# Twenty attention heads in one sequence, the memory rows split by GpSimd, and the recurrence's keys and turns moved

## The reference, cut to what matters

```python
# first block
proj = rms_norm(h) @ w_in                        # attention, gating unit, gates
h = h + merged @ w_out
h = h + hier_moe(rms_norm(h), ...)               # 32 experts of width 256; two for each row
x = rms_norm(h, norm_f_g)
# second block: two layers over x, with a memory of 256 rows
mem_n = rmsnorm(mem, mem_norm_g)
for layer in (0, 1):
    u = rmsnorm(h, norm_g[layer, 0])
    mem_kv = mem_n @ w_mem_kv[layer]
    # layer 0: 16 heads of 64 with a window and a sink; layer 1: a gated recurrence of 8 heads, in chunks of 16
    o = mixer(u)
    c = memory_cross_attn(xq, mem_kv)            # 4 heads of 128, in both layers
    h = h + rmsnorm(concatenate([o, c]) @ w_out)
    h = h + rmsnorm(conv_ffn(rmsnorm(h)))
```

## Time and profile before

| what | value |
|---|---|
| median of 3 runs | 1323.81 us |
| lowest and highest run | 1322.87 and 1324.84 us |
| the profiled execution's own time | 1322.58 us |
| its span, first to last instruction | 1320.9 us |
| instructions | 18486 |
| PE, PEld busy | 1236.1 and 988.4 us |
| POOL, ACT, DVE busy | 770.3, 659.5 and 483.7 us |
| moved by DMA | 275.01 MB |

### The profile page before, as it was taken

The page is one execution under the profiler, slowest core; times in us unless marked ns, Lnnn a source line. Parts: engine busy times, 40 slices in busy tenths (PEclk is TensorE's granted clock), DMA queues, the critical chain, the costliest instruction groups (busy, mean ns, idle before and its releaser), DMA issues.

```text
span 1320.9 us, 18486 instructions
## 1 busy us (share of the span) xinstructions
PE 1236.1 (94%) x7264; PEld 988.4 (75%) x7264; DVE 483.7 (37%) x1084; ACT 659.5 (50%) x1148; POOL 770.3 (58%) x345
## 2 busy tenths in 40 slices
PE   8999999999888778999899999999999889999998
PEld 6888877777343333888788888888998678888986
DVE  2527343433121111456603444102458281344411
ACT  6455544653111011745646666545798443666651
POOL 5778985440000000982176888996688905788894
PEclk8999999998999999999999999999999999999999
DMA  6745554298999999562143655653534413355561
GB/s 210 259 138 187 191 186 159 100 366 334 422 421 375 422 422 413 177 221 81 33 150 113 206 181 184 237 190 128 191 128 169 167 65 128 129 191 192 191 204 67
DMA packets 127037, 275.01 MB, mean 208 GB/s; under 512 B 6580, under 2 KB 55020, under 8 KB 115180
## 3 DMA queue, kind: packets, MB, share of 16 engines
q1 hardware_dynamic: 126668, 272.86, 56.6%
q10 hardware_dynamic: 288, 1.05, 0.2%
HBM read 272.85 MB, written 1.05 MB: 207 GB/s over the span
## 4 chain that ended last, share of the span: by engine, by line
PE 75%; DMA 8%; ACT 7%; DVE 4%; POOL 3%; issue 2%; SPq 1%; DVEq 0%; ACTq 0%; POOLq 0%
PE lin_ps L950 11%; PE lin_ps L952 11%; PE lin_ps L951 11%; DMA ring<-in_w_expert_in 7%; PE lin_ps L1003 6%; PE sc_ps L1268 4%; POOL w_low L877 3%; PE lin_ps L1005 3%; PE tr_ps L1003 3%; PE sc_ps L1003 3%; PE lin_ps L980 2%; PE lin_ps L983 2%; PE lin_ps L982 2%; ACT w_high L1568 2%; PE lin_ps L1088 2%
## 5 line engine op out<-in xcount | busy, mean ns | idle before, releaser
L877 POOL TENSOR_TENSOR w_low<-ring,w_high 128x1024 fp32r<-128x1024 f32 (+1 forms) x318 | 761.0, 2429 | 456.0 <-ACT w_high L1568 456.0
L1568 ACT ACTIVATE w_high<-ring 128x1024 fp32r<-128x1024 f32 (+1 forms) x320 | 313.8, 1043 | 102.1 <-PE lin_ps L952 32.7
L950 PE MATMUL lin_ps<-w_high,x_span 128*128 128x512 f32 (+2 forms) x432 | 168.6, 390 | 5.1 <-POOL w_low L877 2.6
L951 PE MATMUL lin_ps<-w_low,x_span 128*128 128x512 f32 (+2 forms) x432 | 166.2, 385 | 0.0
L952 PE MATMUL lin_ps<-w_high,x_low 128*128 128x512 f32 (+2 forms) x304 | 116.5, 383 | 0.0
L1003 PE MATMUL lin_ps<-x_span,w_high 128*128 128x512 f32 x320 | 112.6, 397 | 1.5 <-ACT work L1598 1.5
L950 PEld LDWEIGHTS lin_ps<-w_high,x_span 128*128 128x128 f32 x432 | 81.7, 189 | 21.8 <-DVE w_low L2115 2.8
L951 PEld LDWEIGHTS lin_ps<-w_low,x_span 128*128 128x128 f32 x432 | 81.8, 189 | 15.2
L980 PE MATMUL lin_ps<-x_span,w_high 128*128 128x256 f32 x320 | 91.4, 286 | 0.0
L982 PE MATMUL lin_ps<-x_span,w_low 128*128 128x256 f32 x320 | 90.5, 283 | 0.0
L1005 PE MATMUL lin_ps<-x_span,w_low 128*128 128x256 f32 x320 | 89.3, 279 | 0.0
(11 more groups left out here) (465 smaller groups left out, 2371.7 us busy)
## 6 DMA issues: line engine op xcount, KB each, us to landing
ring<-in_w_expert_in SPq DMA_DIRECT2D x30, 2048.0 KB, 16.0
ring<-in_ffn_w_in SPq DMA_DIRECT2D x44, 1024.0 KB, 7.4
ring<-in_w_in SPq DMA_DIRECT2D x12, 2048.0 KB, 7.8
ring<-in_b_w_in SPq DMA_DIRECT2D x11, 2048.0 KB, 8.1
work<-in_w_expert_out SPq DMA_DIRECT2D x8, 2048.0 KB, 23.3
ring<-in_w_expert_out SPq DMA_DIRECT2D x8, 2048.0 KB, 22.4
ring<-in_ffn_w_out SPq DMA_DIRECT2D x8, 2048.0 KB, 7.8
ring<-in_a_w_in SPq DMA_DIRECT2D x4, 2048.0 KB, 8.0
```

The source lines that it names most:

```text
L877: pool.tensor_tensor(w_low[:, slot, 0:words], raw, w_high[:, slot, 0:words].bitcast(F32), ALU.subtract).then_inc(low_made, 1)
L950: pe.matmul(out[:, t, :], high(k)[:, at], wh[:, j, :], start=(k == 0), stop=False)
L951: pe.matmul(out[:, t, :], high(k)[:, at], wl[:, j, :], start=False, stop=False)
L1568: act.activation(w_high[:, slot, 0:words], raw, ACT.Copy).then_inc(high_made, 1)
```

## The change

It does four things.

1. **One sequence.** The sixteen heads and the four of cross attention become one sequence of twenty on PE, ACT and DVE. The split of two units moves behind the turn of head 19.
2. **The memory rows.** ACT copies the turned rows in full to one place, `mem_T`. DVE's eight subtractions go. POOL copies `mem_T` to `mem_high` and subtracts, once batch 1's first weights are used, and PE waits for that (`mem_split`) before `kv00`. PE's wait for all eight chunks moves into `w_out1`, ahead of its third chunk. Since `mem_high` isn't there yet, `keep_running` takes `ident` by `ident`, 128 columns, 64 and 26 times. The place of `mem_high` holds one more 1 MB load until then: expert 4's half of batch 1's part a=1, issued ahead of the second half of batch 0's.
3. **The keys.** The fourth level place moves to `gain`. ACT moves the near keys of the first pair before it copies b2 and b3. SP loads the next `gain` only after all sixteen level products, and what stands behind it in SP's queue waits too. PE waits for the block in the banks of the levels first, and for the other one ahead of the chunks.
4. **The turns.** Heads 6 and 7 are turned ahead of chunks 3 and 5 of `o10`.

The diff, cut to its core:

```diff
-        mem_high, mem_low = overlay("mem_high", 6 * 2048, [P, KC, SEQ]), overlay("mem_low", 9 * 2048, [P, KC, SEQ])
+        mem_high, mem_low = overlay("mem_high", 9 * 2048, [P, KC, SEQ]), overlay("mem_low", 6 * 2048, [P, KC, SEQ])
...
+        mem_T = feat(buf(6))
...
-        level_at = [(work, 0), (work, 1024), (attn, 0), (attn, 1024)]
+        level_at = [(work, 0), (work, 1024), (attn, 0), (gain, 0)]
...
+        later_slot = buf(9).rearrange("p (k n) -> p k n", k=4)
...
             def load_gain(src, uses_before):
+                if uses_before == 4:
+                    sp.wait_ge(hg_level_used, len(LEVELS) * HG_HEADS // 2)
...
+                sp.wait_ge(x_low_made, split_groups["merged"] + 8)
+                sp.dma_start(later_slot, io["w_expert_in"][0][BATCH].rearrange("(p k) n -> p k n", k=KC)[:, 4:8, :])\
+                    .then_inc(extra_in, 16)
                 last_use(3)
                 load_first(0, 1, 1)
...
-                firsts_when_free(1, 1, 1)
+                sp.wait_ge(expert_used[1], 1)
+                sp.dma_start(first_slot(1)[:, 1], io["w_expert_in"][0][BATCH + 1].rearrange("(p k) n -> p k n", k=KC)[:, 4:8, :])\
+                    .then_inc(expert_in[1], 16)
+                load_first(1, 1, 1)
...
             pool.wait_ge(expert_used[0], 2)
+            pool.wait_ge(expert_used[1], 2)
+            step(pool.tensor_copy(mem_high[:], mem_T))
+            pool.tensor_tensor(mem_low[:], mem_T, mem_high[:].bitcast(F32), ALU.subtract).then_inc(mem_split, 1)
             step(pool.memset(maskb, 0.0))
...
             turn_split("mem", 8, scaled_mem)
-            parts_made(pe, "mem", 8)
...
                 if k == 2:
+                    parts_made(pe, "mem", 8)
                     pe.wait_ge(h_half, TILES)
...
-                    pe.matmul(lin_out("w_out1")[:, 0, 0:SEQ], mem_high[:, i % KC, 0:P], mem_high[:, i % KC, :], start=True, stop=True)
-
-            keep_running(34)
+                    pe.matmul(lin_out("w_out1")[:, 0, 0:P], ident[:], ident[:], start=True, stop=True)
+
+            keep_running(64)
...
-            keep_running(14)
+            keep_running(26)
...
+            pe.wait_ge(mem_split, 1)
             linear_turned("kv00", *from_mem)
...
+            lin_wait(pe, "kv00")
+            lin_wait(pe, "kv01")
+            name, heads, dim, _, keys, values = crossing(0)
+            attention(*grouped, begun=True, then=(name, heads, dim, first_cross_query, keys, values))
...
-            lin_wait(pe, "b2")
-            lin_wait(pe, "b3")
+            level_block, chunk_block = sorted(("b2", "b3"), key=lambda name: blocks[name][0] % 2)
+            lin_wait(pe, level_block)
...
                 if i >= 2:
                     pe.wait_ge(hg_masked, i - 1)
+                else:
+                    lin_wait(pe, chunk_block)
...
-            for i in range(HG_HEADS - 3, HG_HEADS):
-                turn_head(i)
+            turn_head(HG_HEADS - 3)
+
+            def last_heads(k):
+                if k in (3, 5):
+                    turn_head(HG_HEADS - 2 + (k == 5))
+                parts_made(pe, "o", min(k, HG_HEADS - 1) + 1)
...
-            take_high(act, "mem", 8, mem_high, "mem")
+            for i in range(KC):
+                act.wait_ge(x_turned, split_groups["mem"] + i + 1)
+                act.activation(mem_T[:, i, :], split_ps(i), ACT.Copy, scale=col("mem", i)).then_inc(x_low_made, 1)
+            act.sem_inc(x_high_made, KC)
...
-                                  ATT_HEADS - 1: lambda: split_to(piece("a3") + 2)})
-            attention("attx0", X_HEADS)
+                                  ATT_HEADS + X_HEADS - 1: lambda: split_to(piece("a3") + 2)}, more=X_HEADS)
...
-            for j in range(2):
-                copy_block(f"b{2 + j}", half(hv, j))
-            warm_root()
...
-            pieces_used(act, piece("b3"))
+            act.wait_ge(gain_used, 4)
             act.wait_ge(hg_dec, 2)
             near_keys(0)
+            for j in range(2):
+                copy_block(f"b{2 + j}", half(hv, j))
+            warm_root()
...
-                    take_low(dve, "mem", 8, mem_high, mem_low, "mem")
```

More of the change, by code:

```diff
@@ L399, in program @@
         router_done = sem("router_done")
+        mem_split = sem("mem_split")
         moe_pick = sem("moe_pick")
@@ L1045, in small_out, with attention, scores @@
                 return lin_ps[:, 2 * (o % 2), :]
-            def attention(tag, heads, dim, q, k, v, begun=None):
+            def attention(tag, heads, dim, q, k, v, begun=None, then=None):
                 base = ATT_BASE[tag]
                 z_buf, p_buf, pT_buf = att_bufs1 if tag == "attx1" else att_bufs
-                def scores(i):
-                    g = base + i
+                sequence = [(f"{tag}_{i}", i, dim, q, k, v) for i in range(heads)]
+                if then:
+                    sequence += [(f"{then[0]}_{i}", i, *then[2:]) for i in range(then[1])]
+                def scores(n):
+                    g = base + n
+                    _, i, _, q, k, _ = sequence[n]
                     if g >= 2:
@@ L1075, in attention @@
                 turn_probs(0)
[L1076 to L1081, removed]
+                for place, (name, i, dim, _, _, v) in enumerate(sequence):
+                    g, job = base + place, jobs[tag] + place
+                    if place + 2 < len(sequence):
+                        scores(place + 2)
+                    if place + 1 < len(sequence):
+                        turn_probs(place + 1)
                     pe.wait_ge(tr_moved[job % 2], job // 2 + 1)
-                    out = small_out(pe, f"{tag}_{i}")
+                    out = small_out(pe, name)
                     pT = pT_buf[:, g % 2].rearrange("p c s -> p (c s)")
@@ L1609, in gained, with attention @@
                 return lambda i, ps: act.activation(dst[:, i, :], ps, ACT.Copy, scale=col(name, i))
-            def attention(tag, heads, scaled_sink=None, begun=None, after_turn={}):
+            def attention(tag, heads, scaled_sink=None, begun=None, after_turn={}, more=0):
                 base = ATT_BASE[tag]
@@ L1624, in probs @@
                     ins.then_inc(att_probs, 1)
-                    if scaled_sink:
+                    if scaled_sink and i < heads:
                         act.activation(esink[:, g % 4, :], nmax[:, g % 4, :], ACT.Exp, bias=sink[:, i:i + 1])\
@@ L1633, in attention @@
                         return
-                for i in range(heads):
+                for i in range(heads + more):
                     g = base + i
@@ L1644, in attention @@
                         after_turn[i]()
-                    if i + 2 < heads:
+                    if i + 2 < heads + more:
                         probs(i + 2)
@@ L2064, in rotate, with attention, top @@
                         step(dve.tensor_tensor(y[:, :, a, :], y[:, :, a, :], m, op))
-            def attention(tag, heads, dim, scale, y, mask=None, with_sink=False, begun=None):
+            def attention(tag, heads, dim, scale, y, mask=None, with_sink=False, begun=None, then=None):
                 base = ATT_BASE[tag]
                 z_buf, p_buf, pT_buf = att_bufs1 if tag == "attx1" else att_bufs
-                def top(i):
-                    g = base + i
+                sequence = [(f"{tag}_{i}", i, dim, scale, y, mask, with_sink) for i in range(heads)]
+                if then:
+                    sequence += [(f"{then[0]}_{i}", i, *then[2:], None, False) for i in range(then[1])]
+                def top(place):
+                    g = base + place
+                    _, i, _, scale, _, mask, with_sink = sequence[place]
                     dve.wait_ge(att_scores, g + 1)
-                    if i >= 2:
+                    if place >= 2:
                         dve.wait_ge(att_probs, g - 1)
@@ L2095, in attention @@
                         return
-                for i in range(heads):
-                    g = base + i
-                    if i + 2 < heads:
-                        top(i + 2)
+                for place, (name, i, dim, _, y, _, with_sink) in enumerate(sequence):
+                    g = base + place
+                    if place + 2 < len(sequence):
+                        top(place + 2)
                     dve.wait_ge(att_probs, g + 1)
```

47 lines of the change are left out of this document (27 added, 20 removed).

## The result

The changed kernel takes 1330.73 us (median of 15 runs, 1325.70 to 1335.08), the kernel before 1323.34 us beside it (15 runs, 1320.44 to 1327.38). The ratio is 1.0055, with a 95% interval of 1.0042 to 1.0068: 7.4 us slower, between 5.6 and 9.0. The profiled execution took 1333.70 us, its span is 1332.0 us, 11.1 more than that of before.

What follows compares the result with a forecast made beforehand. The prediction took PE, three quarters of the last-ending chain, as the bound. Terms of +12.1, 0, -2.0, -0.1 and -1.9 gave +8.1 us on the profiled 1322.58, 1330.7; median put at 1331.2, range 1325.5 to 1335.5.

Steps and rivals of the forecast that it cites:

- memory rows: Turns ahead of `w_out1`: PE waits for ACT alone, no longer for DVE's subtractions; -2.4 us, between -1.5 and -3.3.
- first filler: After the router: 64 `ident` calls are 128 instructions, 23 at the low clock level, 16.8 us against 6.38; +10.4 us.
- second filler: Ahead of batch 0: 26 `ident` calls are 52 instructions at 0.112 us, 5.8 us against 1.76; +4.1 us.
- experts: Expert batches: a later first product means an equally later end, and the extra 1 MB counts nothing; 0, bounds -2.5 and 0.
- one sequence: Turn from sixteen heads to cross attention: head 16's scores follow output 13; -2.0 us, between -3.2 and 0.
- near keys: Recurrence, level 1: PE's idle 1.48 us goes, but DVE's next level waits for POOL; -0.1 us, without hold-up -1.5.
- turns: End of the recurrence: `o10` starts after head 5's turn, without PE's 2.08 us wait; -1.9 us, between -1.5 and -2.3.
- The two dry spells: Experts: DMA shares 0.38 at 325 to 330 us and 0.27 at 398 show the stream waiting for PE.
- the stream covers the delay: Rival, experts: bytes alone set their end, so filler and memory rows don't count; 1319.8 us, chance 0.06.
- the one instruction: Rival, fillers: an `ident` product is one instruction, not two; -2.1 us in all, 1321.7 us, chance 0.04.
- The hold-up by POOL that was counted: Recurrence: DVE's next level, with two SBUF operands, waits for POOL until 1055.35; near keys give -0.1, not -1.5 us.
- The hold-up that was a rival: Batch 2: POOL's passes needing 12.1 us, not 9.4, delay DVE's pick and PE by 4.7 us; 1335.9 us, chance 0.07.

Runs made afterwards that it cites:

- x12_wait_back: The changed kernel with PE's wait for all eight copies of the memory rows back ahead of `w_out1`; timeline only, 3.50 us from first turn to `w_out1`.
- x6_mem_back: The changed kernel with memory rows, filler of 34 and 14 products and loads as in the kernel before; 1318.02 us, ratio 0.9949 to the kernel before.
- x11_best_again: The changed kernel with the filler cut to 16 and 6 products and ACT's split of two `o10` units moved later, second measurement; 1314.12 us, ratio 0.9924.
- x3_ident_only: The kernel before with only the new filler, `ident` by `ident`, 64 and 26 times; 1337.29 us, ratio 1.0103 to the kernel before.
- x9_no_extra: The kernel of `x11_best_again` without the extra 1 MB load ahead of batch 0; 1314.03 us, ratio 0.9924 to the kernel before.
- x2_none: The changed kernel with both calls of `keep_running` deleted, so no filler; 1319.50 us, ratio 0.9977 to the kernel before.
- x8: The changed kernel with the last three heads turned ahead of `o10` again; timeline only, 2.2 us more from the second pair's level 4 to `o10`'s ninth chunk.
- x10: The kernel of `x11_best_again` with the memory rows, filler of 34 and 14 products and loads of the kernel before; 1317.27 us, ratio 0.9951.

## Why the prediction was right

It said 1331.2 us, 1325.5 to 1335.5, slower; measured were 1330.73 and +7.4 us where the sum gave +8.1. Every term came within 0.3 us of its forecast. Step by step, from the two profiles:

| step | predicted | measured | from |
|---|---|---|---|
| memory rows | -2.4 | -2.7 | first turn to `w_out1`: 2.24, before 4.92 |
| first filler | +10.4 | +10.3 | count 8.03 us later, `w_out1` 2.31 earlier |
| second filler | +4.1 | +4.1 | gather 12.17 us later, count 8.03 |
| experts | 0 | -0.3 | 11.90 - 12.16 |
| one sequence | -2.0 | -2.2 | 9.72 - 11.90 |
| near keys | -0.1 | -0.3 | second pair's level 4 +10.70, first pair's +11.03 |
| turns | -1.9 | -2.1 | 8.62 - 10.70 |
| sum, before rounding | +8.1 | +6.9 | |

**The filler.** The trace shows the 128 and 52 instructions, and the split into slow and fast ones held: 16.8 us were forecast, and 16.83 passed from the first of them to the count. That this came out to a tenth was luck: the execution of after met the low level for as long as that of before. In `x12_wait_back` the same 128 instructions took 14.54 us, near the bound "all at the high level" (14.3). The loss itself doesn't hang on that luck. From the start of DVE's last part of h to batch 0, with both kernels' clock at 0.76 from 304 to 318 us, it takes 33.23 us (after) and 18.70 (before), 14.5 more; with both at 1.00, 29.98 (`x12_wait_back`) and 16.68 (`x6_mem_back`, with the filler of before), 13.3 more.

**The pass-on.** The two dry spells were the argument, and every profile bears it out: batch 0's first product lies anywhere from 318.15 us (`x11_best_again`) to 337.67 (`x3_ident_only`), but from there to the end of the experts it takes 203.0 to 204.1 us in all fourteen. The rival that the stream covers the delay is out, and so is the one instruction. The 1 MB load was rightly counted as nothing, as far as `x9_no_extra` shows it.

**The hold-up by POOL that was counted** is shown: 2.67 us with POOL busy, 1.42 with POOL moved away. The rule that the prediction weighed, of the Trainium skill, SBUF — State Buffer, "Who interferes with whom", agrees with both. **The hold-up that was a rival**, in batch 2, did not come; its price was mis-sized. The two passes took 1.89 + 4.55 = 6.4 us and not 9.4, since the copy, with one operand, took 0.4 of the subtraction's time. The pick had 5 us to spare:

```profile
367.01 1.89 POOL L922 CAST mem_high<-work 128x2048 fp32r<-128x2048 f32 x1 [87.41 <-PE sc_ps L1295]
368.99 4.55 POOL L923 TENSOR_TENSOR mem_low<-work,mem_high 128x2048 fp32r<-128x2048 f32 x1
...
379.04 0.41 DVE L2409 TENSOR_TENSOR work<-work,iota 128x256 f32<-128x256 f32 x1
```

**The range** was looser than its reasons. Its lower end, "the clock high and half of the better ends", comes to 1331.2 - 2.4 - 1.5 = 1327.3 by the prediction's own terms, not 1325.5, and the hold-up that its upper end of 1335.5 names was priced at 1335.9. The measured time lies inside either.

**What the steps don't explain.** The two profiled executions differ by 11.1 us, not 6.9. Of the other 4.2 us, 0.4 were there at the first turn of the memory rows, 1.3 arise at the start of the first feed-forward, where the granted clock was 0.83 from 714 to 724 us and 1.00 in the same stretch of before, and 2.5 behind `o10`, in the second one. The change touches none of these. The medians differ by 7.4, between 5.6 and 9.0, which agrees with the steps, so I take the 4.2 us for a difference of two executions (below).

## What to carry to other kernels

A filler that keeps an engine running is work in order: price it by the instructions and the clock level that the trace shows, and end it when the result it waits for is there. Longer, it delays all that follows; left out, it costs the clock. Before a delay is called hidden, look for the moments when the other resource, here the DMA stream, stands still and waits for it; and when a wait for one engine is removed, look which third engine holds the next step.

## What the runs showed that was not expected

**The clock's fall after the same pause is not the same in every execution.** In every profile PE stands 1.45 us somewhere between 300 and 308 us, for DVE's h, and in all but that of `x2_none` it then runs the router's products and the filler. In the windows from 304 to 318 us the granted clock of these thirteen was 0.76 or 0.77 in five (before, after, `x8`, `x9`, `x10`), 0.88 in one and 1.00 in seven. Two of them, the changed kernel and `x12_wait_back`, whose code is the same from the router on:

```profile
304.00:318.00 14.00, 14.00 (x97) 13.84 (x96) 6.00 (x30) 7.52 (x13) 0.00 (x0) 0.76 1.01 418
```

```profile
304.00:318.00 14.00, 14.00 (x126) 13.98 (x126) 5.49 (x29) 6.87 (x12) 0.00 (x0) 1.00 1.01 420
```

In the first filler this is 2.3 us (16.83 against 14.54) and in the router's products ahead of it another 1.0, together the 3.25 us between 33.23 and 29.98. The changed kernel's runs lie 9.4 us apart; how much of that comes from here was not measured.

**The feed-forward's products have more than one pace at a granted clock of 1.00.** In windows of 10 us of the last layer's feed-forward, the kernel before, then the changed one: 60 products and 58. Why stays open; no run here was made to tell.

```profile
1230.00:1240.00 10.00, 10.00 (x60) 8.74 (x59) 4.25 (x9) 7.05 (x12) 8.44 (x4) 1.00 0.54 176
```

```profile
1240.00:1250.00 10.00, 10.00 (x58) 8.64 (x58) 3.97 (x8) 6.53 (x11) 8.19 (x4) 1.00 0.50 169
```
